# Prompt half of a sparse-attention layer: column-tiled small projections, streamed compression weights, bias added by TensorE

## What is computed

```python
kv = (rmsnorm(h, norm_kv) @ w_kv).reshape(B, T, KV_SLOTS, N_KV_HEADS, HEAD_DIM)

def compress(rows, pos_emb, w1, w2):          # 64 rows of one head make one block
    blk = rows.reshape(B, nc, BLOCK, KVH, dh) + pos_emb[None, None, :, None, :]
    flat = jnp.transpose(blk, (0, 1, 3, 2, 4)).reshape(B, nc, KVH, BLOCK * dh)
    return jax.nn.silu(flat @ w1) @ w2

s_c = q @ kc + bias(q_pos, cmp_end);  o_c = masked_softmax(s_c) @ vc      # compressed blocks
s_s = q @ k_selected + bias;          o_s = masked_softmax(s_s) @ v_selected
s_w = q @ k_window + bias;            o_w = masked_softmax(s_w) @ v_window
return g[..., 0:1] * o_c + g[..., 1:2] * o_s + g[..., 2:3] * o_w
```

## Time and profile before

| | us |
|---|---|
| median of 3 runs | 2131.95 |
| their range | 2129.97 to 2134.59 |
| profiled execution, its own time | 2129.85 |
| its span, first to last instruction | 2128.1 |

### The profile page before, as it was taken

How to read it: one execution, slowest core, us unless ns; L and a number is a source line. 1 busy time by engine, 2 the same in 40 slices (tenths; PEclk the granted TensorE clock), 3 DMA queues, 4 the chain that set the end, 5 groups by cost and what they waited for, 6 DMA issues and landing times.

```text
span 2128.1 us, 36327 instructions
## 1 busy us (share of the span) xinstructions
PE 1945.2 (91%) x15417; PEld 1562.4 (73%) x15417; DVE 401.2 (19%) x930; ACT 260.1 (12%) x565; POOL 138.1 (6%) x198
## 2 busy tenths in 40 slices
PE   6799998999999978786786999999999999999995
PEld 5589986777767765554566969788796959697882
DVE  3795022000010025543422000000000000000002
ACT  1000011000000114433312000000000000000001
POOL 2071001200000010023201000000000000000001
PEclk9899998999999965678897999999999999999997
DMA  9755655944734224067763979999898979798994
GB/s 243 199 161 161 206 182 175 382 139 138 277 127 111 73 89 167 1 210 254 235 160 115 295 264 343 303 297 311 284 319 277 328 266 340 263 343 304 293 312 162
DMA packets 353746, 484.68 MB, mean 228 GB/s; under 512 B 32548, under 2 KB 310062, under 8 KB 353004
## 3 DMA queue, kind: packets, MB, share of 16 engines
q1 hardware_dynamic: 325600, 392.40, 58.0%
q10 hardware_dynamic: 14924, 45.66, 6.5%
q0 software_dynamic: 13120, 45.15, 6.1%
HBM read 450.51 MB, written 40.98 MB: 231 GB/s over the span
## 4 chain that ended last, share of the span: by engine, by line
issue 46%; PE 42%; DMA 4%; DVE 3%; ACT 2%; another core or an unknown queue 1%; ACTq 1%; POOL 0%; SPq 0%; DVEq 0%; POOLq 0%
PE ps L1415 14%; PE ps L1445 7%; PE ps L1539 4%; PE ps L1561 3%; DMA arena<-in_state_win_kv 3%; PE ps L1580 2%; PE ps L1598 1%; PE ps L1644 1%; PE ps L1722 1%; PE ps L1630 1%; PE ps L1786 1%; PE ps L1383 1%; ACT arena L864 1%; PE ps L1661 1%
## 5 line engine op out<-in xcount | busy, mean ns | idle before, releaser
L1871 PEld LDWEIGHTS ps<-arena 128*128 128x128 f32 x5632 | 633.1, 192 | 5.2 <-issue 5.1
L1871 PE MATMUL ps<-arena 128*128 128x128 f32 x5632 | 633.4, 275 | 1.3 <-ACT arena L899 1.3
L1415 PE MATMUL ps<-arena 128*128 128x288 f32 x1216 | 303.8, 414 | 20.8 <-DMA arena<-in_conv_w_pw 15.7
L1881 PE MATMUL ps<-arena 128*128 128x512 f32 x704 | 304.2, 593 | 1.7 <-DVE arena L1327 1.7
L1415 PEld LDWEIGHTS ps<-arena 128*128 128x128 f32 x1216 | 235.2, 194 | 88.7 <-DMA arena<-in_conv_w_pw 14.9
L1881 PEld LDWEIGHTS ps<-arena 128*128 128x128 f32 x704 | 133.1, 190 | 168.1 <-issue 168.1
L1327 DVE TENSOR_TENSOR arena<-arena,ps 128x256 f32<-128x256 f32 x88 | 37.1, 421 | 883.1 <-ACT arena L915 883.1
L1445 PE MATMUL ps<-arena 64*64 64x128 f32 x4096 | 160.4, 313 | 5.0 <-issue 5.0
L1445 PEld LDWEIGHTS ps<-arena 64*64 64x64 f32 x4096 | 156.1, 248 | 9.0 <-issue 8.4
L1007 DVE SCALAR_TENSOR_TENSOR arena<-arena 128x256 f32<-128x256 f32 x240 | 119.9, 578 | 0.0
L915 ACT ACTIVATE arena<-ps 128x256 f32<-128x256 f32 x88 | 33.8, 384 | 531.1 <-PE ps L1871 531.0
(11 more groups left out here) (298 smaller groups left out, 1161.5 us busy)
## 6 DMA issues: line engine op xcount, KB each, us to landing
arena<-in_moe_w_gate SPq DMA_DIRECT2D x88, 1024.0 KB, 6.5
arena<-in_moe_w_up SPq DMA_DIRECT2D x88, 1024.0 KB, 7.2
arena<-in_moe_w_down SPq DMA_DIRECT2D x88, 1024.0 KB, 4.9
arena<-in_cache_kv SPq DMA_DIRECT2D x176, 256.0 KB, 5.5
arena<-in_cache_kv POOLq DMA_DIRECT2D x80, 256.0 KB, 7.1
xg_scratch<-arena POOLq DMA_DIRECT2D x26, 512.0 KB, 17.6
arena<-in_conv_w_pw SPq DMA_DIRECT2D x12, 1024.0 KB, 14.1
arena<-in_cmp_w ACTq DMA_DIRECT2D x6, 2048.0 KB, 21.8
```

The source lines that it names most:

```text
L1415: ins = mm(dst, w[:, k, c * P:(c + 1) * P], rhs[:, k, :], start=(k == 0), stop=(k == KD - 1))
L1871: ins = mm(dst, w[:, k, c * P:(c + 1) * P], XeT[:, k, :], start=(k == 0), stop=(k == KD - 1))
L1881: ins = mm(ps[:, 4 + c, :], He[:, 2 * k + kk, :], w[:, kk, 512 * c:512 * (c + 1)], start=(k == 0 and kk == 0), stop=(k == 10 and kk == 1))
```

## The change

Four edits, on PE, ACT and DVE.

1. **K/V projection.** The 32 sample rows become four column tiles: each of 8 contraction steps issues four products of 64 columns, one into each quarter of the output partitions (128x32 stationary, all four the same rows). ACT then copies four pieces of 32x64 (in place of one of 32x256).
2. **Compression.** Data and weight change places: 32 columns (2 slots x 4 blocks x 4 heads) of the data are stationary in one of four column tiles, and 128 weight columns move. Half of each product is not used. ACT copies the sums (`part`), two products with a matrix `fold` add the halves and turn them, then Silu and second weight as before, the V side repeated for 16 heads. The buffer of the data is filled by 8 transfers of half the size in place of 4. An early dummy Silu, and an early dummy Exp behind it, load ACT's tables.
3. **Compressed branch for all heads at once.** Block scores of all 16 heads and both query tiles are 16 products of 8 columns into one bank, before the units; one softmax on 128x128 on DVE and ACT, one pair of transposes and one copy. Per unit one product with `Vz` (values of the pair, zero for other heads) adds it to the output.
4. **Attention.** The table is no longer turned upright in advance: in each unit two products per wide or narrow score bank, reversal matrix stationary and table moving, add the bias to the scores in PSUM for both branches at once. DVE finds the maximum in PSUM, ACT reads PSUM for the exponentials. The loop is unrolled, values are multiplied one unit late, and the output alternates between banks 6 and 7. PE waits for `pa_exp` of unit i before scores of i+2, and for `pa_pt` of unit i-1 before transposes of i. The first K/V transfers of the sample attention start with `pco_mm` (the compressed products) in place of `flip_mm`.

The core of the diff:

```diff
@@ PE, K/V projection
-                for t, (t0, n) in enumerate(TILES):
+                for t, (t0, n) in enumerate(TILES[:2]):
...
+                for k in range(KD):
+                    for r in range(4):
+                        ins = mm(ps[32 * r:32 * r + 32, bk + 2, 0:HD], xnT[:, k, TP:T], w[:, k, HD * r:HD * (r + 1)],
+                                 start=(k == 0), stop=(k == KD - 1), skip_group_check=True)
@@ PE, compression
-                    ins = mm(ps[:, kvi, 0:16], w1[:, kvi, d, :], x[:, :, :, d], start=(d == 0), stop=(d == 31))
+            for i in range(16):
+                for kvi in range(2):
+                    for half in range(2):
+                        d, r = 2 * i + half, 2 * kvi + half
+                        ins = mm(ps[32 * r:32 * r + 32, 0, 0:P], x[:, :, d], w1[:, kvi, d, :], start=(i == 0),
+                                 stop=(i == 15), skip_group_check=True)
+            for kvi in range(2):
+                ins = mm(ps[:, 1, 16 * kvi:16 * kvi + 16], part, fold[:, kvi, :], start=True, stop=True)
@@ PE, bias table and block scores
-            for j in range(8):
-                ins = mm(ps[:, j, :], flip, Tflip[:, 2 * j:2 * j + 2, :].rearrange("p a b -> p (a b)"),
-                         start=True, stop=True)
-            ins.then_inc(sem("flip_mm"), 1)
+            for at in range(2 * G):
+                for t in range(2):
+                    ins = mm(blocks[:, t, at // G, :, at % G, :], QT[:, at, t * P:(t + 1) * P], kcTp[:, at // G],
+                             start=True, stop=True, skip_group_check=True)
@@ PE, a unit
+                for q in range(2):
+                    bias = Tflip[:, 8 * pr + 4 * q + g, 2 * P - nk:].unsqueeze(1).to_broadcast([P, 2, nk])
+                    ins = mm(ps[:, 2 * w + q, 0:2 * nk].rearrange("p (b n) -> p b n", b=2), flip, bias, start=False,
+                             stop=True, skip_group_check=True)
...
+            for i in range(4 * G):
+                if i + 2 < 4 * G:
+                    qk(i + 2)
+                trp(i)
+                if i:
+                    pv(i - 1)
+            pv(4 * G - 1)
@@ DVE, a unit
-                v.tensor_tensor(Sp[:, w, :, :, 0:nk],
-                                ps[:, 2 * w:2 * w + 2, 0:2 * nk].rearrange("p q (b n) -> p q b n", b=2),
-                                of_pair(Tb[:, :, 2 * P - nk:], pr, g).to_broadcast([P, 2, 2, nk]), ALU.add)
+                v.tensor_reduce(mp[:, w, :], ps[:, 2 * w:2 * w + 2, 0:2 * nk].rearrange("p q (b n) -> p q b n", b=2), AXX,
+                                ALU.max, negate=True).then_inc(sem("pa_max"), 1)
@@ ACT, a unit
-                        sc.activation(Sp[:, w, q, br, 0:nk], Sp[:, w, q, br, 0:nk], ACT.Exp,
-                                      bias=mp[:, w, i:i + 1], accum_out=sp[:, w, i:i + 1])
+                        ins = sc.activation(Sp[:, w, q, br, 0:nk], ps[:, 2 * w + q, br * nk:(br + 1) * nk], ACT.Exp,
+                                            bias=mp[:, w, j:j + 1], accum_out=sp[:, w, j:j + 1])
```

More of the change, by code:

```diff
@@ L200, in build @@
         w2 = take(2, HD)
-        chid = take(2, 16)
+        chid = take(16)
         CB = cursor[0]
@@ L231, in build @@
         before = take(P)
+        flip = take(P)
         earl8 = take(64)
@@ L802, in _ @@
             act.wait_ge(sem("kct_zero"), 1)
+            sc.activation(small[:, 6:7], ident[:, 0:1], ACT.Silu)
+            act.wait_ge(sem("pcmp_used"), 1)
+            sc.activation(part, ps[:, 0, 0:P], ACT.Copy).then_inc(sem("pch_ready"), 1)
             act.wait_ge(sem("pcmp_used"), 2)
-            for kvi in range(2):
-                ins = sc.activation(chid[:, kvi, :], ps[:, kvi, 0:16], ACT.Silu, bias=pbias[:, kvi:kvi + 1])
-            ins.then_inc(sem("pch_ready"), 1)
+            sc.activation(chid, ps[:, 1, 0:16], ACT.Silu, bias=pbias[:, 0:1])
@@ L816, in pa_exp @@
+            def pa_exp(i):
+                w, nk = i % 2, P * (i % 2 + 1)
+                act.wait_ge(sem("pa_max"), i + 2)
                 for q in range(2):
                     for br in range(2):
-                        i = 2 * q + br
-                        sc.activation(Sp[:, w, q, br, 0:nk], Sp[:, w, q, br, 0:nk], ACT.Exp,
-                                      bias=mp[:, w, i:i + 1], accum_out=sp[:, w, i:i + 1])
-                for q in range(2):
-                    ins = sc.activation(Sc[:, w, q, :], Sc[:, w, q, :], ACT.Exp, bias=mp[:, w, 4 + q:5 + q])
@@ L823, in pa_exp @@
-                ins.then_inc(sem("pa_exp"), 1)
-            def pa_turn(g, last):
-                for u in range(4):
-                    if not (last and u == 3):
-                        pa_exp(g, u + 1)
-                    w, nk = u % 2, P * (u % 2 + 1)
-                    act.wait_ge(sem("pa_tr"), g * 4 + (u + 1))
-                    sc.activation(PTc[:, w], ps[0:4, 7, P:3 * P].rearrange("p (a b) -> p a b", a=2), ACT.Copy)
-                    sc.activation(PTp[:, w].rearrange("p (q i) c -> p q (i c)", q=2)[:, :, 0:2 * nk],
-                                  ps[:, 4:6, 0:2 * nk], ACT.Copy).then_inc(sem("pa_pt"), 1)
@@ L845, in _ @@
+            pa_exp(0)
+            act.wait_ge(sem("pa_tr"), 1)
+            sc.activation(PTc, ps[0:64, 6, 0:2 * P].rearrange("p (a b) -> p a b", a=2), ACT.Copy).then_inc(sem("pa_pt"), 1)
+            for i in range(4 * G):
+                if i + 1 < 4 * G:
+                    pa_exp(i + 1)
+                pa_turned(i)
             act.wait_ge(sem("prompt_done"), 1)
@@ L1158, in pa_turn @@
-            def pa_turn(g, first, last):
-                for u in range(4):
-                    if not (last and u == 3):
-                        if not (first and u == 0):
-                            dve.wait_ge(sem("pa_tr"), g * 4 + u)
-                        if u < 3:
-                            front(g, u + 1)
-                        else:
-                            front(g + 1, 0)
-                    if u == 2 and not last:
-                        queries(g + 1)
-                    back(g, u)
-                    if u > 0:
-                        done(g, u - 1)
-                    elif not first:
-                        done(g - 1, 3)
@@ L1185, in _ @@
+            blocks_in()
+            front(0)
+            blocks_out()
+            for i in range(4 * G):
+                if i + 1 < 4 * G:
+                    front(i + 1)
+                back(i)
+                if i >= 2:
+                    done(i - 2)
+            done(4 * G - 2)
+            done(4 * G - 1)
+            dve.wait_ge(sem("pa_o"), 4 * G)
             v.memset(small[:, 5:6], 0.0).then_inc(sem("prompt_done"), 1)
@@ L1608, in _ @@
+            ins.then_inc(sem("pcmp_used"), 1)
+            pe.wait_ge(sem("pch_ready"), 2)
+            for k in range(NKV):
+                pr, q = divmod(k, 2)
+                mm(ps[64 * q:64 * q + 64, 4, pr * 4:(pr + 1) * 4], w2[:, 0, :], chid[:, k * 4:(k + 1) * 4],
+                   start=True, stop=True)
+                ins = mm(ps[0:64, 5, k * HD:(k + 1) * HD], chidV[:, k].rearrange("p h n -> p (h n)"), w2[:, 1, :],
+                         start=True, stop=True)
             ins.then_inc(sem("pco_mm"), 1)
```

282 lines of the change are left out of this document (127 added, 155 removed).

## The result

| | us |
|---|---|
| the kernel before, median of 4 runs | 2133.27 (2129.97 to 2141.11) |
| the changed kernel, median of 4 runs | 2041.00 (2039.63 to 2047.64) |
| ratio, 95% interval | 0.9579 (0.9555 to 0.9603) |
| profiled execution of the changed kernel, its own time and span | 2039.63, 2037.8 |

The account below looks back on a forecast made before the run. PE's issue was taken to bound the projections, weight loads compression, a three-engine chain the attention. Terms -9.2, -20.2 and -50.6 sum to -80 us, giving a median of 2052; ends 2037 to 2074, stated range 2036 to 2092.

Parts of the forecast that it names:

- the forecast's own case: Whole kernel: PE becomes the attention's bound at full clock, median 2052 us; chance 0.64.
- What bounds: Old kernel: PE's issue bounds the projections, weight loads compression, a unit's chain through three engines the attention.
- K/V projection, -9.2: K/V projection: sample rows' passes replaced by small column-tile passes, -9.2 us (-14.7 to -5.3).
- the price of a small pass: K/V projection: 384 passes of 64 columns at 29 ns each, 11.1 us added.
- The 1.2 us for changes of shape: K/V projection: PE changes its tile shape 12 times, 0.10 us a change, 1.2 us added.
- Compression, -20.2: Compression: 25.2 us of products removed, 5.0 added, chain behind counted even; -20.2 us (-21.5 to -14).
- Attention, -50.6: Prompt attention: PE becomes the bound, 8.6 us a pair, 80.6 us for 131.2; -50.6 (-59 to -39).
- Rival: the clock swings: Attention: late hand-overs open gaps and the clock falls; 100 us for 131.2, total 2071, or 2092; chance 0.18.
- Half clock in the attention: Attention, rival: half clock throughout, 15.6 us a pair, nothing gained, total 2102; chance 0.08.
- Rival: column tiles do not load side by side: Projection and compression: each small pass pays its own 110 ns load; total 2099; chance 0.04.
- Slower: small tiles cost the neighbours' clock: Projections: small passes bring surrounding wide passes to half clock, +85 us; total 2137, or 2188; chance 0.04.
- the marks named beforehand: Changed profile: small passes 25 to 40 ns, K/V stage 54 to 60 us, compression under 6, pairs 8.5 to 9.5.

Follow-up runs that it names:

- the second profile: The changed kernel run once more, unchanged, beside two other variants: 2043.77 us, ratio 0.9589 to the kernel before.

## Why the prediction held, step by step

2041.0 lies 11 below the 2052 forecast, inside the range, and the forecast's own case is the one that came.

- **What bounds.** That PE's issue bounds the projections was right. That a chain through three engines set the old attention's pace is borne out by PE's waits (32.3 us before, 3.2 now) and, for one link, by a run: values on time bring back 14.4 us of waits for ACT's copy, and the attention grows by 13.4.
- **K/V projection, -9.2 for -16.4: the term that was mis-sized.** The failed step is the price of a small pass. I took 29 ns of the earlier trace rows "since the tile is the same"; it was 16.1, near the lower end that I had worked out from half the columns (5.6 us; measured 6.2). The runs with 32 columns (10.9 ns) and with one tile at a time (48.6) say why: with four tiles side by side the columns are the price, and I had held the tile's shape for it. The 1.2 us for changes of shape was a misreading: a change does cost time, but the kernel before already made the same twelve, since its sample rows ran in 128x32 tiles, so nothing is added. The copies behind the last product, 0.4 estimated, cost 0.56 more than before. Of the 7.2 us missed, 4.9 are the passes (11.1 - 6.2) and 1.2 the shape changes; about 1 is luck, the start of the stage, at full clock in this profile and not in others: the second profile's stage took 52.0.
- **Compression, -20.2 for -21.6.** The sum was near with a wrong term in it. For columns that lie 64 apart I took 39 ns (5.0 us). At full clock the 128 passes take 4.24 us, 33 ns by the row, where the row gives 29; whether the spacing makes these 4 ns no run isolates. In the first profile half clock over its first 63 passes made 5.67 of it. The chain behind it, which I held for even, took 3.2 us (from 734.35 to the block scores at 737.54) for 5.2: the other 2 us.
- **Attention, -50.6 for -51.0.** The pair was put at 8.6 and took 8.45; by parts, narrow and wide, scores 1.71 (predicted 1.92), bias 2.80 (2.63), transposes 1.48 (1.86), values 1.62 (1.70), block values 0.84 (0.5). The block scores took 5.7 (6.3), the first two units 7.4 where the same rows give 4.5 at full clock, so +2.9 (+2.3), and 80.2 less these (67.6 + 5.7 + 2.9) leaves 4.0 for hand-overs and tail (3). So the way of counting held, by rows of single passes at a known clock; that the sum is met within 0.4 us is in part luck, since errors of both signs cancel. DVE at 32.18 of 52 us, 5.2 a pair, and ACT at 30.98, 5.0, came as put (5.6 and 5.2).
- **Rival: the clock swings.** Refuted for the changed kernel. I had read the earlier trace rows as gaps that lower the clock; with gaps of 0.69 and 1.11 us put back it stayed 1.00 at 82% busy. The waits of the old attention were longer in part (up to 5.0 us), and no run put those back, so why its clock swung stays open. Half clock in the attention was limited to its start: 0.55 over 738 to 748, block scores and first units.
- **Rival: column tiles do not load side by side.** Refuted by 16.1 ns a pass beside loads of 106 to 110 ns. The Trainium skill (TensorE: Matmul & The Clock Gate, Part 3: Packing small matmuls — row/col tiling) lists that a load overlaps running products only if its row group differs, though the same part also lets a load into a background weight buffer run ahead; here all four tiles share the rows, so the first rule alone does not hold in this case, and no run tells whether the second is the reason. The measurement decides: even with one tile at a time a pass takes 48.6 ns, under half of its load's row.
- **Slower: small tiles cost the neighbours' clock.** Refuted: 1.00 over the projection and the query projection. Some profiles of the changed kernel start the projection at half clock, as the kernel before did.

Of the marks named beforehand three came out a little better than put: the small passes (16.1 ns for 25 to 40), the K/V stage (50.4 us for 54 to 60) and the pair (8.45 us for 8.5 to 9.5).

Shown by runs: the late values' share, what scores and bias cost in the attention, the tiles' side by side work, the orientation of compression. Argued only, from rows: that the reading of the scores by DVE and ACT straight from PSUM costs nothing (an exponential of 256 columns takes 478 ns for the 496 of the earlier trace rows, a wide maximum 1225 for 1222); no run put the copy back. Open: how the attention's other 37.6 us divide between the table, DVE's work that is gone and the clock, which was 0.62 over 783 to 905.6 and is 0.94 over the attention now; why the clock fell in the tail of the run with two maxima, and what the compression's clock hangs on from one execution to the next.

## What to carry to other kernels

Price a small matrix product by its columns and by what stands beside it: order column tiles so that neighbours differ, and take the price from a row with the same number of columns, not only the same tile. When an attention's pace is set by hand-overs, count whether PE's own work could cover them if products were put one unit late; if it could, the time is the sum of PE's passes, and that sum can be made to a few per cent from rows at a known clock. Before you add a price for something new, such as a change of tile shape, look at the shapes of the kernel before: a merged row can hide that it is already paid. A filler that covers one wait is often the cover of another: look what stands behind the place that it leaves.

## What was not expected of the hardware

- Passes in four 32-column tiles, in turn, by their rows: 10.9 ns for 32 columns, 16.1 for 64, 29 to 33 (compression) for 128. The same passes with one tile after the other: 48.6 for 64 columns, 102 for 128, beside load records of 110 and 133 ns.
- A change between 128x128 and 128x32 tiles is not free: 32 wide passes between two changes take 7.11 us, where their distance inside the run, 216 ns, makes 6.91. Twelve such changes stand in the projection of both kernels.
- The granted clock did not follow PE's busy share: 1.00 with 57.14 busy of 70 us (values on time), 0.50 with 24.00 busy of 24 (compression as before, passes of 16 columns), and it rose from 0.50 to 0.97 in the middle of the compression's passes of 128 columns.
